# Feed-forward stages: GpSimd starts its scaled inputs with the stage, instead of after the last low part of the normed inputs

## The chip, the cores and the metric

The kernel runs on one core of a Trainium2 chip. The metric is the time of one execution on the device, in microseconds (us), lower is better. A core has five engines that run side by side, each through its own list of instructions: TensorE (PE in the profile; PEld is its weight load) for matrix products, VectorE (DVE) and ScalarE (ACT) for element-wise work, GpSimd (POOL) for element-wise work too, and SyncE (SP), which here issues the transfers. They wait for each other by semaphores: an instruction adds to one when it is done, another engine waits until it has reached a value.

## What is computed

Two small language-model blocks in sequence, on 512 tokens plus 16 learned ones (528 in the first block), width 1024, all in float32. The change concerns the feed-forward part, which comes twice, once in each of the two layers of the first block (hidden width 4096, `ff_up` and `ff_down` of each layer):

```python
for layer in range(DEPTH):                       # DEPTH = 2
    hn = rms_norm(h, attn_norm[layer])
    mix = gated_deltanet(...) if layer == 0 else mlstm(...)
    h = h + mix
    h = h + squared_relu_mlp(rms_norm(h, ffn_norm[layer]), ff_up[layer], ff_down[layer])
...
def squared_relu_mlp(h, w_up, w_down):
    a = jax.nn.relu(h @ w_up)
    return (a * a) @ w_down
```

A third block (gates, attention, one more projection) follows and gives the output.

## The kernel before

The program is a sequence of stages, each a block with one instruction list per engine and a barrier at its end: load and transpose the tokens, the first mixer (three stages), feed-forward 0 (called with name ffn0), the second mixer, feed-forward 1 (ffn1), the last block. Features lie on the 128 partitions, tokens along the free dimension, so `h` is 8 tiles of 128 x 528 (128 x 512 from feed-forward 1 on, where the 16 learned tokens are dropped).

Products keep float32 accuracy with three passes: every operand x is split into a high part (ScalarE copies it to a shorter format, `xhi`) and a low part (VectorE subtracts, `xlo` = x - `xhi`), and TensorE computes whi·xhi + whi·xlo + wlo·xhi.

Both feed-forward stages are `up_down` (line 284), with n = 8 groups of 512 hidden features. For group 0 the up product is plain: two weight units (256 columns each), each times all 8 tiles of the normed input (`unit_tiles`, matmuls of line 196). From group 1 on it is done by a scheme of 7 block products in place of 8 (forms f = 0 to 6 in `up_form`, matmuls of line 663): weight blocks and inputs are first added and subtracted. The mixed inputs are made once per stage: GpSimd multiplies `h` by the gain, tile by tile (line 372, eight instructions, each 128 x 528), and then makes four sums and differences of half blocks (lines 375, 378, 381, 384, each twice as long; each waits for the one before). ScalarE takes their high parts (`t_high`, line 397), VectorE their low parts (`t_low`, line 511). Forms 2, 3, 4 and 6 of the first weight unit need them.

What stands around it at the start of the stage, engine by engine, in the order of each list:

- ScalarE: eight high parts of the gained input (line 938), two squares (941), the high part of weight unit 1 (158), the norm's logarithm and exponential (946, 949), then `cast_up(0,0)`, `cast_up(0,1)` (405), two openings from PSUM (715), a square and a high part of hidden tile 0 (431, 434), `cast_up(0,2)`, `cast_up(0,3)`, the same for hidden tile 1, `t_high` of forms 2, 3, 4, two more openings, `cast_up(0,4)`, `t_high(6)`, `cast_up(0,5)`, square and high part of hidden tile 2, and then `keep` (line 426), which copies the first form's result out of PSUM.
- VectorE: eight low parts of the gained input (line 954), three sums of the norm (962), the low part of weight unit 1 (165), four weight sums (545 to 553), and then thirteen instructions of which four are the low parts of the mixed inputs: `low_up` twice (513), scaling of hidden tiles 0 and 1 (726, twice), low part of hidden tile 0 (557), `low_up` twice, low part of hidden tile 1, `t_low` of 2, 3 and 4, `low_up`, `t_low(6)`. Then comes the scaling of hidden tile 2 (line 726, the third of its kind).
- TensorE: group 0's two units (line 196, with four matmuls of line 970 for the norm between the seventh and eighth input tile of the first), then the forms. Form 2 waits for the low part of its mixed input, form 3 for that and for `keep` of form 0:

```python
if f in (3, 5, 6):
    pe.wait_ge(s.kept, 8 * g + 4 * ub + {3: 1, 5: 2, 6: 3}[f])
```

GpSimd's list of this stage holds nothing but the twelve instructions named. Its results `y` lie in memory that `ahi` and `alo` use from group 1 on. Its inputs are `h` and the gains, both complete before the stage begins. The first line of its list waits until all eight low parts of the normed inputs (`norm.lo`, counted up by line 954) are done.

Of the kernel before, what the change touches and what calls it, by code (L numbers as in the profile page):

```python
# [25 lines left out]
KD = D // P  # L26
# [257 lines left out]
def up_down(k, name, n, up_cols, w_down, activate, acc, norm, then, last_norm):  # L284
# [8 lines left out]
    with ExitStack() as ctx:  # L293
# [54 lines left out]
        @block.sync  # L348
        def _(sp):
            def down(g, j):  # L350
                return wide(w_down, g * 512, 512 * j)
            norm.sync(k, sp)
            def first():
                for j in range(loaded, 2):
                    load_unit(k, sp, u0 + j, up_cols(0, j), (u0 + j) % RAW_SLOTS)
            def step(g, par):
                for j in range(2):
                    if not (zero(g) and 2 + j < loaded):
                        load_unit(k, sp, step_unit(g) + j, up_cols(g + 1, j), slot(j))
                for j in range(2):  # L360
                    load_unit(k, sp, step_unit(g) + 2 + j, down(g, j), slot(2 + j))
            def last():
                for j in range(2):
                    load_unit(k, sp, step_unit(n - 1) + j, down(n - 1, j), slot(j))
            steps(sp, n, step, first, last)
            load_ahead(k, sp, u0 + 4 * n, then)

        @block.gpsimd
        def _(pool):
            pool.wait_ge(norm.lo, KD)  # L370
            for t in range(KD):
                pool.tensor_scalar((y_low if t < 4 else y_high)[:, t % 4, k.now], norm.src[:, t, k.now],
                                   norm.gain[:, t:t + 1], None, ALU.mult).then_inc(s.y_made, 1)
            pool.wait_ge(s.y_made, KD)
            pool.tensor_tensor(y_low[:, :, first_half], y_low[:, :, second_half], y_low[:, :, first_half], ALU.subtract)\
                .then_inc(s.t_made, 1)
            pool.wait_ge(s.t_made, 1)
            pool.tensor_tensor(y_low[:, :, second_half], y_high[:, :, second_half], y_low[:, :, second_half], ALU.subtract)\
                .then_inc(s.t_made, 1)
            pool.wait_ge(s.t_made, 2)  # L380
            pool.tensor_tensor(y_high[:, :, second_half], y_high[:, :, second_half], y_low[:, :, first_half], ALU.subtract)\
                .then_inc(s.t_made, 1)
            pool.wait_ge(s.t_made, 3)
            pool.tensor_tensor(y_high[:, :, first_half], y_high[:, :, second_half], y_high[:, :, first_half], ALU.subtract)\
                .then_inc(s.t_made, 1)
# [4275 lines left out]
```

## Time and profile before

| | |
|---|---|
| time, median of 3 runs | 1918.23 us (1918.07 to 1919.24) |
| profiled execution, its own time | 1919.47 us |
| its span, first to last instruction | 1917.8 us |
| TensorE busy | 1834.2 us, 96% of the span |
| VectorE busy | 1261.2 us, 66% |
| ScalarE busy | 965.0 us, 50% |
| GpSimd busy | 167.5 us, 9% |
| mean granted TensorE clock | 0.980 of full |
| feed-forward 0 begins | at 613.7 us of the span |
| feed-forward 1 begins | at 1233.0 us |

The profile gives, for one execution, when each instruction began and how long it lasted; idle time before an instruction stands in square brackets with the instruction that ended it. Full TensorE clock is 2.4 GHz, the lower level is 1.2 GHz. A duration includes the time in which an instruction that has begun is held up.

### The profile page before, as it was taken

The page shows a single profiled execution, that of the slowest core. Times are in us where ns is not written, and L with a number is a line of the kernel's source. Part 1 is how long each engine was busy: PE and PEld are TensorE (multiplying, and loading weights), DVE is VectorE, ACT ScalarE, POOL GpSimd, SP SyncE. Part 2 cuts the span into 40 slices and gives each one's busy share as a digit, 9 for nine tenths or more (in the row PEclk, how much of TensorE's full clock was granted, in tenths as well). Part 3 has the DMA queues.
Part 4 walks back from the last instruction along what each step waited for, and adds up shares of the span by engine and source line. Part 5 has one row for each costly group of instructions (what it writes and reads, how often), then busy time and mean ns, then how long its engine had stood idle before and what let it go on. Part 6 is the DMA issues. An engine that isn't in the chain of part 4 may idle for free. (4 is left out here: it accounts for less than half of the span.)

```text
span 1917.8 us, 33607 instructions
## 1 busy us (share of the span) xinstructions
PE 1834.2 (96%) x13026; PEld 1671.9 (87%) x13026; DVE 1261.2 (66%) x2235; ACT 965.0 (50%) x1787; POOL 167.5 (9%) x166
## 2 busy tenths in 40 slices
PE   7999999999899799999999999979999998999998
PEld 7999999899699799999999977768889985788776
DVE  6666689986744777777664276567777757863444
ACT  6557763667733544444444366364444433424662
POOL 0001140000000500000000020140000002000101
PEclk9999999999999899999999999989999998999999
DMA  8223462255442133233232232223332332321101
GB/s 203 85 77 118 127 196 59 71 150 164 113 99 67 50 105 111 88 95 103 89 90 89 64 86 79 89 65 107 105 93 88 110 110 68 111 67 45 45 23 44
DMA packets 209652, 179.61 MB, mean 94 GB/s; under 512 B 42544, under 2 KB 181808, under 8 KB 209512
## 3 DMA queue, kind: packets, MB, share of 16 engines
q1 hardware_dynamic: 209512, 177.68, 31.4%
q8 instruction: 95, 1.56, 0.3%
q14 instruction: 45, 0.37, 0.1%
HBM read 164.10 MB, written 13.54 MB: 93 GB/s over the span
## 5 line engine op out<-in xcount | busy, mean ns | idle before, releaser
L196 PE MATMUL ps<-ffn_alo,main_whi 128*128 128x264 f32 (+1 forms) x768 | 205.7, 322 | 0.0
L196 PE MATMUL ps<-ffn_ahi,main_wlo 128*128 128x264 f32 (+1 forms) x768 | 205.1, 321 | 0.0
L196 PE MATMUL ps<-ffn_ahi,main_whi 128*128 128x264 f32 (+1 forms) x768 | 204.7, 321 | 0.0
L196 PE MATMUL ps<-gdn_xhi,gdnf_whi 128*128 128x264 f32 x768 | 160.4, 290 | 4.2 <-DVE gdnf_wlo L1558 4.2
L513 DVE TENSOR_TENSOR main_wlo<-raw,main_whi 128x512 fp32r<-128x512 f32 x212 | 145.0, 686 | 24.8 <-ACT main_whi L405 13.5
L196 PE MATMUL ps<-gdn_xlo,gdnf_whi 128*128 128x264 f32 x768 | 156.1, 285 | 0.0
L196 PE MATMUL ps<-gdn_xhi,gdnf_wlo 128*128 128x264 f32 x768 | 156.0, 284 | 0.0
L575 DVE TENSOR_TENSOR h<-h,ps 128x528 f32<-128x528 f32 (+1 forms) x128 | 89.0, 696 | 88.1 <-PE ps L196 87.5
L165 DVE TENSOR_TENSOR main_wlo<-raw,main_whi 128x2048 fp32r<-128x2048 f32 x38 | 88.1, 2320 | 80.5 <-ACT main_whi L158 80.5
L196 PEld LDWEIGHTS ps<-ffn_ahi,main_whi 128*128 128x128 f32 x768 | 127.8, 188 | 11.2
L196 PEld LDWEIGHTS ps<-ffn_alo,main_whi 128*128 128x128 f32 x768 | 127.5, 188 | 11.0
L196 PEld LDWEIGHTS ps<-ffn_ahi,main_wlo 128*128 128x128 f32 x768 | 127.5, 188 | 10.9
L663 PE MATMUL ps<-ffn_xhi,main_wlo 128*128 128x264 f32 (+1 forms) x448 | 126.5, 282 | 0.0
L663 PE MATMUL ps<-ffn_xhi,main_whi 128*128 128x264 f32 (+1 forms) x448 | 126.2, 282 | 0.0
L663 PE MATMUL ps<-ffn_xlo,main_whi 128*128 128x264 f32 (+1 forms) x448 | 126.2, 282 | 0.0
L196 PEld LDWEIGHTS ps<-gdn_xhi,gdnf_whi 128*128 128x128 f32 x768 | 120.7, 190 | 5.5 <-DVE gdn_xlo L1545 4.4
L1447 DVE SCALAR_TENSOR_TENSOR gdn_y<-gdnf_pre,gdnf_convw,gdn_y 128x528 f32<-128x528 f32 x96 | 82.6, 862 | 59.4 <-ACT gdn_y L1420 57.1
L196 PEld LDWEIGHTS ps<-gdn_xlo,gdnf_whi 128*128 128x128 f32 x768 | 119.6, 189 | 0.0
L196 PEld LDWEIGHTS ps<-gdn_xhi,gdnf_wlo 128*128 128x128 f32 x768 | 119.3, 189 | 0.0
L663 PE MATMUL ps<-ffn_thi,main_whi 128*128 128x264 f32 (+1 forms) x336 | 97.0, 289 | 21.9 <-ACT wide L426 20.4
L405 ACT CAST main_whi<-wide 128x512 fp32r<-128x512 f32 x112 | 69.3, 621 | 81.1 <-PE ps L196 81.0
L405 ACT CAST main_whi<-raw 128x512 fp32r<-128x512 f32 x84 | 52.0, 621 | 107.3 <-PE ps L196 107.2
(556 smaller groups left out, 4909.4 us busy)
## 6 DMA issues: line engine op xcount, KB each, us to landing
raw<-in_ff_up_dram SPq DMA_DIRECT2D x32, 1024.0 KB, 5.5
raw<-in_ff_down_dram SPq DMA_DIRECT2D x32, 1024.0 KB, 5.0
raw<-in_gdn_in_dram SPq DMA_DIRECT2D x24, 1024.0 KB, 6.0
raw<-in_w_in_dram SPq DMA_DIRECT2D x14, 1024.0 KB, 5.3
raw<-in_mlstm_in_dram SPq DMA_DIRECT2D x12, 1024.0 KB, 5.2
raw<-in_gdn_out_dram SPq DMA_DIRECT2D x8, 1024.0 KB, 6.6
gdn_zr<-gdn_z_spilled SPq DMA_DIRECT2D x26, 264.0 KB, 3.0
gdn_v_spilled<-gdn_o SPq DMA_DIRECT2D x16, 264.0 KB, 2.3
```

The lines of the kernel that those rows point to most:

```text
L165: eng.tensor_tensor(k.wlo[:, s, :], k.raw[:, slot, :], k.whi[:, s, :].bitcast(F32), ALU.subtract).then_inc(k.lo_done, 1)
L196: mm = pe.matmul(ps[:, b, 0:k.width], w, x[:, half], start=first and n == 0, stop=last and n == 2)
L405: nc.scalar.copy(whi[:, i % 8, :, :], up_weights(ub, f)).then_inc(k.hi_done if f == 6 else s.hi_part, 1)
L513: return dve.tensor_tensor(wlo[:, i % 8, :, :], src, whi[:, i % 8, :, :].bitcast(F32), ALU.subtract)
L575: dve.tensor_tensor(parted(k, acc[:, j, k.now]), parted(k, acc[:, j, k.now]), filled(k, k.ps[j % 4]), ALU.add).then_inc(s.down_free, 1)
L663: mm = pe.matmul(bank(ub, f), w[:, i % 8, kt, :], y[:, kt, :], start=f in (0, 1, 2, 4) and kt == 0 and x == 0, stop=kt == KD // 2 - 1 and ...
L1447: dve.scalar_tensor_tensor(out=self.y[:, b, :], in0=self.pre[:, b, i:i + T], scalar=self.w[:, i, j:j + 1], in1=self.y[:, b, :], op0=ALU.mu ...
```

## The change

GpSimd's list in both feed-forward stages loses its first line, the wait. Everything else, on every engine, stays.

```diff
         @block.gpsimd
         def _(pool):
-            pool.wait_ge(norm.lo, KD)
             for t in range(KD):
                 pool.tensor_scalar((y_low if t < 4 else y_high)[:, t % 4, k.now], norm.src[:, t, k.now],
                                    norm.gain[:, t:t + 1], None, ALU.mult).then_inc(s.y_made, 1)
```

## Rows read from the trace of the kernel before

**Rows 1.** The page: TensorE's busy share and granted clock, tenths in 40 slices.
```profile
PE   7999999999899799999999999979999998999998
PEclk9999999999999899999999999989999998999999
```

**Rows 2.** Waits in 612 to 722 and 1231 to 1341: total us, times, longest.
```profile
PE ps L663 <- ACT wide L426: 10.3, 1, 10.3
...
PE ps L663 <- ACT wide L426: 10.1, 1, 10.1
```

**Rows 3.** Timeline, feed-forward 0, ScalarE: start, us, instructions, [idle before <-releaser].
```profile
613.73 5.13 ACT L938 ACTIVATE ffn_xhi<-h,gains 128x528 fp32r<-128x528 f32 x8 [10.24 <-PEq L99]
...
646.75 1.07 ACT L397 CAST ffn_thi<-ffn_y 128x1056 fp32r<-128x1056 f32 x1 [4.89 <-POOL ffn_y L381]
...
656.02 0.37 ACT L426 COPY wide<-ps 128x264 f32<-128x264 f32 x1
```

**Rows 4.** Timeline, feed-forward 0, GpSimd.
```profile
620.11 18.08 POOL L372 TENSOR_SCALAR ffn_y<-h,gains 128x528 f32<-128x528 f32 x8 [276.90 <-DVE ffn_xlo L954]
638.28 2.47 POOL L375 TENSOR_TENSOR ffn_y<-ffn_y 128x1056 f32<-128x1056 f32 x1
...
643.37 3.35 POOL L381 TENSOR_TENSOR ffn_y<-ffn_y 128x1056 f32<-128x1056 f32 x1
646.79 2.41 POOL L384 TENSOR_TENSOR ffn_y<-ffn_y 128x1056 f32<-128x1056 f32 x1
```

**Rows 5.** Timeline, feed-forward 0, VectorE.
```profile
614.49 5.52 DVE L954 SCALAR_TENSOR_TENSOR ffn_xlo<-h,gains,ffn_xhi 128x528 fp32r<-128x528 f32 x8 [1.06 <-ACT ffn_xhi L938]
...
622.50 2.28 DVE L165 TENSOR_TENSOR main_wlo<-raw,main_whi 128x2048 fp32r<-128x2048 f32 x1
624.70 1.11 DVE L545 TENSOR_TENSOR wide<-raw 128x512 f32<-128x512 f32 x1
625.74 0.68 DVE L547 TENSOR_TENSOR wide<-raw 128x512 f32<-128x512 f32 x1
...
630.53 1.29 DVE L513 TENSOR_TENSOR main_wlo<-raw,main_whi 128x512 fp32r<-128x512 f32 x2 [2.48 <-ACT main_whi L405]
...
641.89 2.52 DVE L511 TENSOR_TENSOR ffn_tlo<-ffn_y,ffn_thi 128x1056 fp32r<-128x1056 f32 x1 [5.09 <-ACT ffn_thi L397]
...
652.83 1.26 DVE L511 TENSOR_TENSOR ffn_xlo<-ffn_y,ffn_xhi 128x1056 fp32r<-128x1056 f32 x1 [0.28 <-ACT ffn_xhi L397]
654.01 1.32 DVE L726 TENSOR_TENSOR wide<-wide,rinv 128x528 f32<-128x528 f32 x2
```

**Rows 6.** Timeline, single GpSimd scalings of line 372: held up, and alone.
```profile
622.11 4.06 POOL L372 TENSOR_SCALAR ffn_y<-h,gains 128x528 f32<-128x528 f32 x1
...
628.39 1.60 POOL L372 TENSOR_SCALAR ffn_y<-h,gains 128x528 f32<-128x528 f32 x1
```

**Rows 7.** Timeline, first mixer: VectorE's three-operand form alone, and beside GpSimd.
```profile
34.87 0.77 DVE L1447 SCALAR_TENSOR_TENSOR gdn_y<-gdnf_pre,gdnf_convw,gdn_y 128x528 f32<-128x528 f32 x1
...
37.16 1.46 DVE L1447 SCALAR_TENSOR_TENSOR gdn_y<-gdnf_pre,gdnf_convw,gdn_y 128x528 f32<-128x528 f32 x1
```

**Rows 8.** Timeline, feed-forward 0, TensorE: norm, and after the gap.
```profile
627.26 1.05 PE L970 MATMUL ps<-wide,ones 128*128 128x264 f32 x4
...
656.53 0.56 PE L663 MATMUL ps<-ffn_thi,main_whi 128*128 128x264 f32 x1 [10.32 <-ACT wide L426]
```

**Rows 9.** Stretch of 10 us: busy us by engine, PEclk, DMA share, GB/s.
```profile
652.00:662.00 10.00, 5.47 (x30) 5.50 (x31) 9.69 (x16) 7.20 (x15) 0.00 (x0) 0.57 0.05 10
```

**Rows 10.** Timeline, feed-forward 1: GpSimd, VectorE (line 513, then 726).
```profile
1239.29 18.11 POOL L372 TENSOR_SCALAR ffn_y<-h,gains 128x512 f32<-128x512 f32 x8 [76.66 <-DVE ffn_xlo L954]
...
1248.94 1.29 DVE L513 TENSOR_TENSOR main_wlo<-raw,main_whi 128x512 fp32r<-128x512 f32 x2 [1.82 <-ACT main_whi L405]
...
1272.78 1.28 DVE L726 TENSOR_TENSOR wide<-wide,rinv 128x512 f32<-128x512 f32 x2
```

**Rows 11.** Timeline, start of the second mixer: GpSimd's first instruction.
```profile
986.34 0.20 POOL L3095 MEMSET ml_below<- 128x128 f32 x1 [337.13 <-POOLq L99]
```

## Prediction before the result

> **What bounds the kernel now.** I read the page first: TensorE is busy in nearly every slice at full clock, so only a stretch in which TensorE stands still can give time; in the 40 slices apart from the first, the busy digit dips to 7 in the 14th (623 to 671 us) and in the 27th (1247 to 1294 us) [rows 1]. These are the first tens of microseconds of feed-forward 0 and of feed-forward 1. Second, who waited for whom in the 110 us behind each start: TensorE stood still once for 10.3 us and once for 10.1 us, each time before a form of line 663, until ScalarE's copy of line 426 [rows 2]. Nothing else of this size stands in those stretches. Third, the timelines there, followed backwards from the end of the gap. TensorE resumes with form 3 at 656.53 [rows 8]. It needs `keep` of form 0, which begins at 656.02 [rows 3]. The form that it copies was ready long before; `keep` is late since it stands in ScalarE's list behind the square of hidden tile 2, which waits for VectorE's third scaling of line 726 at 654.01, and that stands in VectorE's list behind the low parts of the four mixed inputs, the last at 652.83 [rows 5]. Those follow ScalarE's high parts, and the one at 646.75 had waited 4.89 us for GpSimd's line 381 [rows 3]. GpSimd works without a pause from 620.11 to the end of line 384 at 649.20, and before 620.11 it waits for the last low part of line 954 [rows 4]. So the wait that is taken out does stand at the head of the chain that ends TensorE's gap, in both stages.
>
> **The start of GpSimd.** Without the wait GpSimd begins with the stage. ScalarE begins at 613.73 [rows 3]; at the start of the second mixer GpSimd's first instruction is at 986.34, level with the others [rows 11]. I take 613.8, which is 6.3 us before 620.11. In feed-forward 1 the scalings begin at 1239.29 [rows 10]; by the same distance behind the block's start at 1233.0 I take 6.2 us. If nothing stood in the way, TensorE's form 3 would come as much earlier: 12.5 us in all. That is the far end, not the forecast, because GpSimd's work moves on top of VectorE's.
>
> **What GpSimd and VectorE cost each other.** A scaling alone takes 1.60 us; another, begun at 622.11, took 4.06 [rows 6], and it ends 1.4 us after VectorE's 2.28 us subtraction of line 165 has ended [rows 5]. Behind that subtraction, the sum of line 545 took 1.11 us where the next, of the same size, took 0.68 [rows 5]. So a scaling waits until VectorE's running instruction has ended, and then holds up VectorE's next one by 1.11 - 0.68 = 0.43 us, not by its whole 1.60. With two inputs it is more: the low part at 641.89 took 2.52 us, the like one at 652.83 took 1.26; it began while GpSimd still ran line 378, and line 381 behind it took 3.35 us in place of 2.47 [rows 4, 5]. They take turns, one instruction each. The three-operand form of line 954, beside which GpSimd never runs in these stages, takes its turn too: the same form in the first mixer took 1.46 us beside a GpSimd sum, 0.77 alone [rows 7].
>
> The Trainium skill, "SBUF — State Buffer", section "Who interferes with whom", says that a VectorE instruction with two SBUF inputs and a GpSimd instruction that reads SBUF exclude each other for the whole instruction. The rows for GpSimd's sums agree (a wait until the other has ended), the row for the scalings does not: 0.43 us of hindrance for 1.60 us of instruction. Read literally for the scalings too, the rule speaks against this change; that is the third rival below.
>
> **The scalings, moved.** The first runs before VectorE has anything to do (613.8 to 615.4). The others meet the eight low parts, one per 5.52 / 8 = 0.69 us [rows 5]. Each waits for the end of the running one, holds up the next by 0.43, and comes back 1.6 us later, so to a boundary at 0.43 + 2 x 0.69 = 1.8 us; behind them come the norm's sums and the 2.28 us of line 165, which costs one of them up to 2 us more. Bounds for eight: 8 x 1.8 = 14.4 us, and the 18.08 of today [rows 4]. I take 16.3, nearer to the middle, since one long wait is sure: scalings done at 630.1, where they end at 638.2 now.
>
> VectorE pays at most 7 x 0.43 = 3.0 us for these, about 1 of which it pays already. Its four weight sums end at 628.05 now (630.53 less 2.48 of idle [rows 5]), so at 630.0 then, and its next instruction, which waits for ScalarE, is at 630.53: hidden, with 0.5 us left; without that cover 1 us at most would be lost. TensorE needs the norm's sums at 627.26 [rows 8] (now ended before 622.5, where line 165 begins [rows 5]) and line 165 about 2 us later (now ended at 624.78): 2 us later each is hidden as well. TensorE's first unit wants a low part every 1.5 us (12 matmuls of 0.12), and 0.69 + 0.43 = 1.1 us is less. The very first low part at 614.49 could be held up by the end of GpSimd's first read: 0 to 0.43 us at TensorE's start, taken as 0 because the scaling has been reading for 0.4 us by then.
>
> **From 630.5 on VectorE is what counts.** From the first line 513 to the third scaling of line 726 it has 13 instructions: nine of 128 x 528 or less at 0.62 us from start to start, and four low parts of mixed inputs at 1.17 (durations 0.65 and 1.26 less the overlap with the next). That is 9 x 0.62 + 4 x 1.17 = 10.3 us; it takes 654.01 - 630.53 = 23.5 us now, the rest being waits for GpSimd's results. With the change GpSimd's four sums fall into this stretch from its beginning, and each takes its turn between two of VectorE's. What a sum holds is bounded by 1.9 us (2.47 less half a microsecond until it reads) and 2.4 us (2.41 and 2.47 whole [rows 4]); I take 2.3, the row of line 384 being the nearest. Sum: 10.3 + 4 x 2.3 = 19.5 us, less 0.3 for the part of the first sum before 630.53. The third line 726 is then at 630.53 + 19.2 = 649.7 in place of 654.01: 4.3 us earlier. GpSimd's last sum is done near 642 (630.1 + 4 x 2.45 + 4 x 0.6 of turns), and ScalarE's remaining high parts and copies take 4 us from there: they do not come last. From line 726 to form 3 it stays 656.53 - 654.01 = 2.5 us. So form 3 starts at 652.2. Form 2 waits a little longer than now for its first low part, which changes nothing, since form 3 ends the gap.
>
> In feed-forward 1 the same: nine at 0.605 and four at 1.14 make 10.0 us, four sums of 128 x 1024 at 2.25 make 9.0. From 1248.94 this gives 1267.9, in place of 1272.78 [rows 10]: 4.8 us earlier.
>
> **Sum.** 4.3 + 4.8 = 9.1 us. All that follows in these stages hangs on TensorE, on weight buffers that TensorE frees, or on loads that these release, so it moves as a whole, and later stages begin at a barrier. TensorE's clock: in 652 to 662 it was granted 0.57 of full after the gap [rows 9], which is the 1.2 GHz level for some 4 us, and cost about 2 us; with a gap of 5 to 6 us I expect that again and count nothing. The profiled execution takes 1919.47 us, so it would take 1910.4; that execution lay 1.2 us above the median of the runs shown, 1918.23, which gives 1909.1.
>
> **Rivals.**
> First, the full shift. GpSimd and VectorE hinder each other less than in rows 4 and 5, or the shorter gap spares the drop of the clock: 12.5 us without hindrance, up to 4 more by the clock, so 1902 to 1906. For it speaks only that half of GpSimd's scalings would find VectorE's list short; against it the turns seen in each of GpSimd's overlaps. Chance 0.12.
>
> Second, GpSimd is locked out: the eight low parts of line 954 follow each other without a gap, and if GpSimd does not get a turn between them, only the first scaling (1.6 us) is won, per stage. That is 3.2 us: 1915.0, hardly to be told from no change. Against it: at the end of line 165 VectorE had the next instruction ready as well, and GpSimd did get its turn [rows 5, 6]. That the change does nothing because GpSimd starts late for another reason would look the same. Chance 0.08.
>
> Third, the slower side: a scaling holds VectorE for its whole 1.60 us, from the first low part on. It decides where a low part plus a scaling takes longer than the 1.5 us that TensorE spends per input tile; at 0.69 + 1.60 = 2.3 us it would. The eighth low part would then be at 614.5 + 8 x 2.3 = 632.9; sums of the norm, line 165 and the weight sums add 1.9 + 2.2 + 2.4, then 10.3 + 9.2: the third line 726 at 658.9, 4.9 us later than now, in both stages. 1928. The Trainium skill's rule above, taken for the scalings too, gives this. Against it the 0.43 us of line 545. Chance 0.04.
>
> **Chances and range.** The forecast with its terms has 0.73, the first rival 0.12, the second 0.08, the third 0.04, and 0.03 is left for the unforeseen. The bounds: with 1.9 us per sum of GpSimd the gain is 9.1 + 8 x 0.4 = 12.3; with 2.4, scalings of 18 us and 1 us lost at each start it is near 5. I take 1905.0 to 1914.4. A measurement can tell about 0.2% from no change, 3.8 us, so faster means below 1914.4. Faster 0.87 (forecast, first rival, a part of the rest), same 0.08, slower 0.05.
>
> **What would show it.** Line 372 begins within 0.3 us of the stage, its eight instructions take 15 to 18 us, and several instructions of line 954 last about 1.2 us. The four sums begin near 630 and each is followed by one lengthened VectorE instruction of 513, 726 or 557. The third line 726 is near 649.7 and 1267.9, and TensorE's wait for line 426 shrinks from 10.3 to about 5 us. Wrong would be: TensorE waiting in its first unit for line 954, or the third line 726 where it is now; then the turns cost what the start gave.

## The result

| | before | changed |
|---|---|---|
| median | 1918.15 us (1917.11 to 1920.92, 6 runs) | 1906.68 us (1905.08 to 1912.48, 6 runs) |
| profiled execution, its own time | 1919.47 us | 1905.67 us |
| its span | 1917.8 us | 1904.0 us |
| mean granted clock | 0.980 | 0.986 |

The ratio is 0.9945, with a 95% interval of 0.993 to 0.9961: 11.5 us faster by the medians, 7.5 to 13.4 us by the interval. 9.1 had been forecast, and a time of 1905.0 to 1914.4 us. One execution of the kernel before, beside the last experiments, took 3593.21 us and is left out of their comparisons.

**Where it went, by stage.** The start of a stage is the start of ScalarE's first or GpSimd's first instruction in it; the differences, in us, from the profiled executions:

| | before | changed |
|---|---|---|
| feed-forward 0, start to start of the second mixer | 372.6 | 368.7 |
| second mixer (not changed) | 246.7 | 243.9 |
| feed-forward 1 | 365.0 | 360.2 |
| behind feed-forward 1 (not changed) | 319.8 | 317.3 |

3.9 + 4.8 = 8.7 us lie in the two stages that were changed, and 2.8 + 2.5 = 5.3 in code that the change does not touch; the experiments come back to these.

**Feed-forward 0 after the change.** GpSimd's timeline; lines of the file are one less than before. It answers to [rows 4].

```profile
613.83 17.50 POOL L371 TENSOR_SCALAR ffn_y<-h,gains 128x528 f32<-128x528 f32 x8 [271.35 <-POOLq L99]
631.41 2.81 POOL L374 TENSOR_TENSOR ffn_y<-ffn_y 128x1056 f32<-128x1056 f32 x1
634.30 2.81 POOL L377 TENSOR_TENSOR ffn_y<-ffn_y 128x1056 f32<-128x1056 f32 x1
...
640.10 2.82 POOL L383 TENSOR_TENSOR ffn_y<-ffn_y 128x1056 f32<-128x1056 f32 x1
```

GpSimd begins with the stage (ScalarE's first instruction is at 613.80). Each sum lasts 2.82 us in place of the 2.47 or less that one takes alone, and behind it follows the next at once.

VectorE's timeline in the same place (answers to [rows 5]):

```profile
614.57 6.79 DVE L953 SCALAR_TENSOR_TENSOR ffn_xlo<-h,gains,ffn_xhi 128x528 fp32r<-128x528 f32 x8 [1.07 <-ACT ffn_xhi L937]
...
630.59 1.29 DVE L512 TENSOR_TENSOR main_wlo<-raw,main_whi 128x512 fp32r<-128x512 f32 x2 [1.21 <-ACT main_whi L404]
631.80 5.88 DVE L725 TENSOR_TENSOR wide<-wide,rinv 128x528 f32<-128x528 f32 x2
637.60 2.98 DVE L556 TENSOR_TENSOR ffn_alo<-wide,ffn_ahi 128x528 fp32r<-128x528 f32 x1
640.51 3.56 DVE L512 TENSOR_TENSOR main_wlo<-wide,main_whi 128x512 fp32r<-128x512 f32 x2
...
644.61 3.58 DVE L510 TENSOR_TENSOR ffn_tlo<-ffn_y,ffn_thi 128x1056 fp32r<-128x1056 f32 x3
...
649.88 1.31 DVE L725 TENSOR_TENSOR wide<-wide,rinv 128x528 f32<-128x528 f32 x2
```

The eight low parts cost 6.79 us in place of 5.52. From 630.59 on VectorE is never idle: the two scalings that took 1.75 us together now take 5.88, because two of GpSimd's sums take their turns there, and two more sit in the next two rows. The third scaling is at 649.88.

TensorE in feed-forward 0, the matmul after each idle stretch among the forms (answers to [rows 8]), and its longest wait in 1225 to 1335, feed-forward 1 (answers to [rows 2]):

```profile
645.95 0.36 PE L662 MATMUL ps<-ffn_thi,main_whi 128*128 128x264 f32 x1 [1.48 <-issue]
...
652.40 0.56 PE L662 MATMUL ps<-ffn_thi,main_whi 128*128 128x264 f32 x1 [4.75 <-ACT wide L425]
```

```profile
PE ps L662 <- ACT wide L425: 4.2, 1, 4.2
```

The gap of 10.3 us has become one of 4.75 and a new one of 1.48 ahead of form 2, in feed-forward 1 4.2 and 2.8 in place of 10.1 and 1.4. (Where a row says "issue", the profile shows nothing that the engine waited for; form 2's code waits there for its low part, the first of the three at 644.61.)

### The profile page after: what moved, and what is told of

Its sections match the earlier page's. It is cut to its first block and busy times, and to the rows that moved or that the text cites. A ratio compares the mean times of both kernels' runs of the same rounds, so it can differ in the third digit from the quotient of the medians.

```text
span 1904.0 us, 33607 instructions
## 1 busy us (share of the span) xinstructions
PE 1826.9 (96%) x13026; PEld 1665.8 (87%) x13026; DVE 1273.9 (67%) x2235; ACT 963.8 (51%) x1787; POOL 167.1 (9%) x166
## 3 DMA queue, kind: packets, MB, share of 16 engines
q1 hardware_dynamic: 209512, 177.68, 31.7%
## 5 line engine op out<-in xcount | busy, mean ns | idle before, releaser
L512 DVE TENSOR_TENSOR main_wlo<-raw,main_whi 128x512 fp32r<-128x512 f32 x212 | 144.9, 685 | 21.2 <-ACT main_whi L410 10.3
```

The source lines that it names most:

```text
L512: return dve.tensor_tensor(wlo[:, i % 8, :, :], src, whi[:, i % 8, :, :].bitcast(F32), ALU.subtract)
```

## The experiments

**The changed kernel again, and the wait taken out in one layer alone.** What would separate the change's own gain from the 5.3 us in unchanged code.

> The changed kernel once more. In its first profiled execution the span was 13.8 us shorter than that of the kernel before, of which 3.9 lie in feed-forward 0, 4.8 in feed-forward 1, and 5.1 in the stages behind them, which are unchanged. Theory A (turns on VectorE): the change is worth 8 to 9 us, in the feed-forward stages; the rest are drops of TensorE's clock to 1.2 GHz that fall in some executions and not in others. Then the median is 8 to 12 us below the kernel before, feed-forward 0 again gives 3.8 to 4.3 us from its start to the start of the next stage, and some of the 5 us in the unchanged stages is gone or moved elsewhere. Rival B: the unchanged stages gain by the shift itself; then the start of the second mixer to the start of feed-forward 1 is again 244.0 us (246.7 before) and feed-forward 1's end to the end of the program again 2.5 us shorter than before.

```diff
         @block.gpsimd
         def _(pool):
+            if last_norm:
+                pool.wait_ge(norm.lo, KD)
             for t in range(KD):
```

> The wait is taken out in feed-forward 0 alone and stays in feed-forward 1. Theory A: feed-forward 0 is as in the changed kernel (third scaling of hidden tiles about 36 us behind the stage's start, TensorE's gap there 4.8 us), feed-forward 1 as in the kernel before (39.7 us behind its start, gap 10 us); the time is 4 to 5.5 us below the kernel before, 1913 to 1914.5. Rival B (the unchanged stages gain by being shifted): 6 to 8 us below, since the second mixer and the last block are shifted too.

| | feed-forward 0 | second mixer | feed-forward 1 | behind it |
|---|---|---|---|---|
| changed, again | 368.6 | 244.4 | 360.4 | 319.8 |
| layer 0 alone | 368.7 | 244.1 | 364.5 | 319.8 |

Medians, with the runs of the kernel before on the same chip at 1919.44: changed again 1908.9 (ratio 0.9937, 0.9923 to 0.9951), layer 0 alone 1913.24 (0.9966, 0.9953 to 0.9979). The feed-forward stages repeat to 0.2 us. The part behind them is back at 319.8, so its 2.5 us were no gain of the change. The second mixer stays near 244, which still fits both theories. Nor does the time tell them apart: 6.2 us by the medians lies where rival B had it (6 to 8) and above theory A's 4 to 5.5, and its interval, 4.0 to 9.0 us, holds both. With the wait back in feed-forward 1 that stage is at 364.5; its third scaling comes 39.4 us behind its start (39.7 before), its gap ahead of form 3 is 9.8 us. Half of the change is there: 3.9 us in feed-forward 0. The second mixer's 246.7 - 244.1 adds 2.6.

**The kernel before twice more, and the changed one a third time.** Files unchanged; only the question of the second mixer.

> The kernel before, profiled again. The two feed-forward stages took 372.6 and 365.0 us in its first profile, the second mixer 246.7, and the part behind feed-forward 1 319.8. If drops of TensorE's clock are what makes the unchanged stages differ between executions (theory C), the feed-forward stages repeat within 1 us, and the second mixer and the last part may come out at 244 or 317.3 as they did in an execution of the changed kernel, each difference going with one more or one less stretch at 1.2 GHz. If instead the change itself makes the second mixer shorter (rival B), it is 246.7 again.

> The kernel before, a third profile, for the same question: theory C, feed-forward stages 372.6 and 365.0 within 1 us, the second mixer either 244 or 246.7 according to the clock; rival B, 246.7.

> The changed kernel, a third profile. Feed-forward 0 368.6 and feed-forward 1 360.3 us within 0.5, VectorE's third scaling of hidden tiles 36.1 us behind the start of feed-forward 0. Theory C: the second mixer 244 or 246.7 according to the clock; rival B: 244 again.

| | feed-forward 0 | second mixer | feed-forward 1 | behind it | time |
|---|---|---|---|---|---|
| before, again | 372.4 | 246.7 | 364.9 | 319.8 | 1919.39 |
| before, third | 372.5 | 246.7 | 364.9 | 319.8 | 1921.48 |
| changed, third | 367.9 | 246.7 | 360.9 | 320.0 | 1913.44 |

Rival B had said 246.7 for the kernel before, and so it came; but the changed kernel's third execution has the second mixer at 246.7 too, so a shift of the stage does not by itself make it shorter: rival B falls. (Its feed-forward 0, 367.9, is 0.2 us outside what was expected; the third scaling is 36.0 us behind the start.) The whole second mixer in the changed kernel's first profile and in its third (columns: us, busy us of PE, PEld, DVE, ACT, POOL, granted clock, DMA share, GB/s):

```profile
982.54:1226.47 243.93, 234.83 (x1494) 204.24 (x1494) 131.46 (x305) 118.43 (x248) 19.59 (x24) 0.99 0.30 84
```

```profile
984.17:1230.83 246.66, 237.58 (x1494) 206.84 (x1494) 131.23 (x305) 118.90 (x249) 17.60 (x24) 0.98 0.30 83
```

The same 1494 matmuls kept TensorE busy for 2.75 us longer, and the stage is 2.73 us longer: the difference is TensorE's clock. It sits in two places. In the ten microseconds that begin 135 us and 165 us behind the mixer's start the granted clock was 0.83 in the third profile, as in the kernel before, and 1.00 in the first; 0.83 over 10 us is 3.4 us at 1.2 GHz and full clock otherwise. Behind feed-forward 1 it is the same: TensorE was busy for 304.3 us in the kernel before and for 301.8 in the changed kernel's first profile, with 1764 matmuls in both.

That the kernel before showed 246.7 in all three of its profiles was allowed by theory C but not what it would lead one to expect. The experiments below add to the count. Of the eight profiles in which GpSimd begins with feed-forward 0, five have the mixer at 243.9 to 244.4, one at 245.2 and two at 246.7 and 246.8; the four in which it begins later (the three of the kernel before, and the half-way one) have 246.7 each. So the change may make these two drops rarer, which would be worth more than the 8.7 us; these profiles are too few to settle it.

**GpSimd's sums made narrow.** How much of what is left is their turns on VectorE?

```diff
+            first_few, second_few = (slice(x.start, x.start + 16) for x in (first_half, second_half))
             pool.wait_ge(s.y_made, KD)
-            pool.tensor_tensor(y_low[:, :, first_half], y_low[:, :, second_half], y_low[:, :, first_half], ALU.subtract)\
+            pool.tensor_tensor(y_low[:, :, first_few], y_low[:, :, second_few], y_low[:, :, first_few], ALU.subtract)\
                 .then_inc(s.t_made, 1)
...
```

> The four sums of GpSimd are made over 16 columns of each half block only; the rest of the mixed inputs is left uncomputed. Scalings as in the changed kernel. Theory A (VectorE's list plus GpSimd's turns is the bound): without the four turns of about 2.3 us, VectorE's third scaling in feed-forward 0 comes at 644 to 645.5 in place of 649.9 (then limited by ScalarE, whose opening of hidden tile 3 waits for TensorE until 641.4), and TensorE's gap ahead of form 3 falls from 4.8 us to 1 to 2.5 us. If the sums cost VectorE nothing (rival: only the order of GpSimd's results counts), the third scaling comes no earlier than 649, because VectorE's and ScalarE's lists are unchanged.

This kernel leaves most of the mixed inputs uncomputed and ran once (1895.46 us); only its timeline is of use.

The stage begins at 616.34 here. VectorE's third scaling, and TensorE's matmul after its only gap of the forms:

```profile
645.98 1.32 DVE L726 TENSOR_TENSOR wide<-wide,rinv 128x528 f32<-128x528 f32 x2
...
648.50 0.36 PE L663 MATMUL ps<-ffn_thi,main_whi 128*128 128x264 f32 x1 [1.57 <-ACT wide L426]
```

645.98 - 616.34 = 29.6 us behind the start, where the changed kernel has 36.1: 6.4 us earlier, half a microsecond beyond the expected 644 to 645.5, which are 30.2 to 31.7 behind 613.8. VectorE's and ScalarE's lists are the same, so the rival (only the order of results counts) falls. But not all of the 6.4 us is the sums. VectorE's first line 513 began at 631.85, 15.5 us behind the start in place of 16.8; from there to the third scaling it is 14.1 us in place of 19.3, so the sums cost 5.2 us net. Their four turns came to 9.0; without them VectorE stands idle for 2.75 us in this stretch, waiting for ScalarE.

The other 1.3 us are the clock's. It stayed at 2.4 GHz (1.00 granted over 615 to 625 and over 645 to 655) through the 2.7 us of idle TensorE at the stage's start and through the gap of 1.57. TensorE makes the norm's column sums early in the stage, ScalarE's work on them stands ahead of its casts of the weight blocks, and VectorE's line 513 waits for the first cast. With 1.00, 0.83 and 0.66 granted over the first ten microseconds of feed-forward 0 that line began 15.2 (the half-way kernel), 16.8 (before, changed) and 18.0 us (the last experiment) behind the start. Feed-forward 0 took 360.1 us, 8.6 less than in the changed kernel: 4.7 of gap (4.75 + 1.48 - 1.57) and 4.0 by the clock, for TensorE was busy for 355.5 us in place of 359.4. Feed-forward 1 took 350.6.

**GpSimd begins half-way.**

```diff
         @block.gpsimd
         def _(pool):
+            pool.wait_ge(norm.lo, 4)
             for t in range(KD):
```

> GpSimd's first wait comes back, but for four low parts instead of eight, so GpSimd begins some 3.6 us behind the stage's start instead of 6.4 (before) or 0.1 (changed). Theory A (VectorE's own 10.3 us and GpSimd's four turns fill the time up to the third scaling of line 726): as long as the sums begin before VectorE runs dry, the start of GpSimd hardly matters; the third scaling comes 36.8 to 37.3 us behind the stage's start (40.3 before, 36.1 changed). Rival (the gain follows GpSimd's start in proportion): 38.3 us or later.

```profile
618.26 19.48 POOL L372 TENSOR_SCALAR ffn_y<-h,gains 128x528 f32<-128x528 f32 x8 [276.06 <-DVE ffn_xlo L954]
637.83 2.47 POOL L375 TENSOR_TENSOR ffn_y<-ffn_y 128x1056 f32<-128x1056 f32 x1
```

```profile
653.56 1.32 DVE L726 TENSOR_TENSOR wide<-wide,rinv 128x528 f32<-128x528 f32 x2
```

I was wrong here: the third scaling is at 653.56 - 614.59 = 39.0 us behind the start, not at 37. GpSimd began 2.7 us earlier than before but its scalings took 19.5 us, not 17.5, and its sums began only when VectorE had run dry (its low part at 641.44 came after 5.09 us of idle time). From the first sum to the third scaling it is 15.73 us, to the hundredth what it was before (638.28 to 654.01). The time is in the rival's range (38.3 or later), but the gain did not follow GpSimd's start in proportion either: that would be 38.5 (2.7 of 6.4 us of lead, so 1.8 of 4.2). So there are two bounds: GpSimd's first sum plus 15.7 us, and VectorE's serial list with the turns. Of the change's 4.2 us, the last half of GpSimd's lead brought 2.9; VectorE's list was the bound with the whole of it and not with the half. The kernel ran once, in 1917.61 us.

**The sums held back.** Are the turns a waste?

```diff
             pool.wait_ge(s.y_made, KD)
+            pool.wait_ge(s.lo, 2)
```

> The changed kernel, but GpSimd's first sum waits until VectorE has made the low part of hidden tile 1, so that no sum takes a turn among the eight instructions ahead of that. Theory A: the turns are work that has to be done anyway on a shared path, and keeping them out of a busy stretch only puts VectorE's idle time behind it: the sums begin 22.3 us behind the stage's start (24.5 before, 17.6 changed), the third scaling comes 2 to 2.5 us earlier than before, 38 us behind the start, which is later than the changed kernel's 36.1. Rival (the turns cost more than they give, the change throws time away there): the third scaling at 36 us or less.

```profile
636.85 2.47 POOL L375 TENSOR_TENSOR ffn_y<-ffn_y 128x1056 f32<-128x1056 f32 x1 [5.66 <-DVE ffn_alo L557]
```

```profile
633.73 0.71 DVE L557 TENSOR_TENSOR ffn_alo<-wide,ffn_ahi 128x528 fp32r<-128x528 f32 x1 [0.76 <-ACT ffn_ahi L434]
...
652.61 1.32 DVE L726 TENSOR_TENSOR wide<-wide,rinv 128x528 f32<-128x528 f32 x2
```

The third scaling is at 652.61 - 613.67 = 38.9 us behind the start, 2.9 later than in the changed kernel and 1.3 earlier than before (2 to 2.5 had been expected, since I took the start of the sums 0.9 us too early). VectorE's early instructions are short again (0.71 us for line 557 in place of 2.98) and it pays with idle time later. The rival falls: to let the sums take turns is worth 2.9 us. 15.76 us lie between the first sum and the third scaling, nearly the 15.73 of before. The kernel ran once, in 1912.8 us.

**ScalarE's copy moved forward.** If `keep` is late only by its place in the list, it can be moved.

```diff
                 cast_up(0, 5)
+                keep(0, 0, 0, 0, 1, 1)
                 squared(0, 2)
                 hi_tile(0, 2, 0)
...
-                    if ub < 2 and f == 0:
+                    if ub < 2 and f == 0 and not (zero(g) and ub == 0):
                         keep(g, ub, f, 0, 1, 1)
```

> The changed kernel, and in addition ScalarE copies the result of the very first form out of PSUM (keep) before the square and the high part of hidden tile 2 instead of behind them, in both stages. If the reading of the chain is right (keep is late only because of its place in ScalarE's list, behind a square that waits for VectorE), form 3 starts at 647.5 in place of 652.4 and the 4.8 us gap ahead of it vanishes; VectorE's list is unchanged, so TensorE then waits ahead of form 5, whose low part VectorE makes at 653.6: a gap of about 3.5 us there. Net 2 to 2.5 us per stage, plus up to 2 if the clock stays up: 4 to 7 us below the changed kernel. Rival: form 3 does not move, because something else holds it (its mixed input or its weight's low part); then the time is that of the changed kernel.

```profile
645.69 0.36 PE L663 MATMUL ps<-ffn_thi,main_whi 128*128 128x264 f32 x1 [1.46 <-issue]
...
654.39 0.56 PE L663 MATMUL ps<-ffn_xhi,main_whi 128*128 128x264 f32 x1 [4.01 <-ACT wide L425]
```

```profile
653.87 0.37 ACT L425 COPY wide<-ps 128x264 f32<-128x264 f32 x1
```

The gap ahead of form 3 is gone (it begins at 647.23), and one of 4.01 us stands ahead of form 5. What ended it was not VectorE's low part, as expected, but ScalarE again: form 5 waits for `keep` of form 2 too, which ended at 654.24, and the low part of its weight block, begun at 653.39, had ended at 654.07. That copy stands in ScalarE's list behind the square of hidden tile 3. In feed-forward 0 this gave only 0.4 us (368.3): over 652 to 662 the granted clock was 0.66, in the changed kernel 0.73. In feed-forward 1 the gap ahead of form 5 was 2.28 us, the clock over 1256 to 1266 was 0.83 against 0.60, and it gave 2.3 us (357.9). The median is 1905.43 (1904.73 to 1906.8), against 1908.9 for the changed kernel on the same chip; ratio to before 0.9924, 0.9912 to 0.9937. The intervals of the two overlap (0.9923 to 0.9951), so that it beats the changed kernel is not shown: it is 3.5 us by these medians, less than the 4 to 7 expected, and 1.3 against the changed kernel's first median, 1906.68.

**Both lists in TensorE's order.** The work is the same, its order is what TensorE asks for.

```diff
+                cast_up(0, 2)
+                cast_up(0, 3)
                 squared(0, 0)
                 hi_tile(0, 0, 0)
-                cast_up(0, 2)
-                cast_up(0, 3)
...
                 cast_up(0, 5)
+                keep(0, 0, 0, 0, 1, 1)
+                cast_up(0, 6)
+                keep(0, 0, 2, 1, 2, 3)
+                for m in range(2, 4):
+                    open_tile(m)
...
                 t_low(6, 4)
+                low_up(0, 5)
+                low_up(0, 6)
+                lo_tile(0, 0, 0)
+                lo_tile(0, 1, 0)
```

> The changed kernel with the lists of ScalarE and VectorE at the start of the stage in the order in which TensorE asks: weight blocks 2 and 3 before the squares, the copies of forms 0 and 2 and the high part of block 6 before the openings of hidden tiles 2 and 3, and VectorE's low parts of blocks 5 and 6 before the low parts of hidden tiles 0 and 1 and the scalings. The work is the same. Theory A: the bound is VectorE's serial list with GpSimd's turns, so what comes last is what stands last: no gap over 1 us ahead of forms 3, 5 and 6; the next wait is ahead of the second unit's first form, which needs 18 short and 4 long instructions and four turns, 11.0 + 4.7 + 9.2 us behind 630.6, 655.5 in place of 660.5 in the changed kernel. 4 to 5 us less per stage: 8 to 10 us below the changed kernel. Rival: ScalarE's list becomes what comes last, and no more is won than with the copy alone moved (2 to 3 us in all).

TensorE's matmuls after idle time, in a stage that begins at 618.60, and the copy that ended the longest wait:

```profile
654.61 0.36 PE L670 MATMUL ps<-ffn_thi,main_whi 128*128 128x264 f32 x1 [1.28 <-DVE main_wlo L517]
...
662.76 0.36 PE L670 MATMUL ps<-ffn_xhi,main_whi 128*128 128x264 f32 x1 [3.55 <-ACT wide L425]
```

```profile
662.25 0.37 ACT L425 COPY wide<-ps 128x264 f32<-128x264 f32 x1
```

The expectation failed, and what it named as its rival is what the rows show. There is a gap of 1.07 us ahead of form 2 (at 651.62), one of 1.28 ahead of form 3 and one of 3.55 ahead of form 6, 5.9 in all where the changed kernel has 6.2; none stands ahead of the second unit. (By count of the matmuls, twelve to a form: form 5 begins at 657.60, form 6 at 662.76.) Form 6 waits for `keep` of form 3, which is ScalarE's copy at 662.25; it was left behind the squares and high parts of hidden tiles 2 and 3, which wait for VectorE's scalings, now later in its list (the third one 39.4 us behind the start). The first form of the second unit begins at 664.56, 46.0 us behind the start, where 41.7 had been expected and the changed kernel has 46.7.

The profiled execution is moreover not a typical one. It took 1915.9 us; of the six executions, only one was longer (1917.11), and the other four lie at 1902.84 to 1906.85. It had feed-forward 0 at 369.3 us and feed-forward 1 at 361.3, both a little more than the changed kernel; the first ten microseconds of both were granted 0.66 of the clock, where the changed kernel had 0.83 and 1.00. The median is 1906.61, ratio 0.9933 (0.991 to 0.9955). The 8 to 10 us did not come, and the order alone is not shown to be worth anything over the copy moved forward.

## Why the prediction was right, point by point

- **The bound and the chain.** Right. TensorE's gap was ended by `keep`, `keep` by the third scaling, that by VectorE's list. From the third scaling to form 3 it is 652.40 - 649.88 = 2.5 us as said, and moving `keep` moved form 3 from 652.40 to 647.23.
- **GpSimd's start.** Right. 613.83 measured, 613.8 said; in feed-forward 1 GpSimd begins level with the block too.
- **The cost of a scaling to VectorE.** Right. The three low parts that were held up lasted 1.12 to 1.21 us against 0.76, so 0.36 to 0.45 us each (0.43 said), and all eight 6.79. What the Trainium skill's "Who interferes with whom" in "SBUF — State Buffer" says of the whole instruction holds here, nearly, for the two-input sums (2.25 us for 2.47 of instruction), and not for the one-input scalings (0.36 to 0.45 for 1.60). The third rival, built on that, is refuted by the same rows.
- **The scalings.** 17.5 us, 16.3 said: the range was 14.4 to 18.1. They ended at 631.33, so no part of the first sum lay ahead of VectorE's stretch, where 0.3 us had been counted. They were 1.2 us late and it did not matter, since VectorE still had work of its own when the first sum came.
- **VectorE's list from 630.5.** 649.88 - 630.59 = 19.3 us; 19.2 said. With 10.3 us of its own the four turns come to 9.0, 2.25 each; 2.3 said. (The prediction's lower bound for a turn, 1.9, takes off half a microsecond "until it reads"; no run shows that half microsecond.) The third scaling: 649.88 against 649.7. In feed-forward 1 34.4 us behind the start, 34.9 said; 35.0 in the third profile, where the clock fell at the stage's start as in the kernel before (0.83 over the first ten microseconds, 1.00 in the first profile).
- **The sum.** 4.3 + 4.8 = 9.1 said for the two stages, 3.9 + 4.8 = 8.7 measured, and 8.6 and 8.8 with the changed kernel's second and third profiles against the same first profile before (8.3 and 8.6 against the second and third). Form 3 came 4.2 us earlier behind the start of feed-forward 0 (38.6 for 42.8) and the stage gave 3.9: after the shorter gap the matmuls ran at 1.2 GHz for 4.8 us (652.40 to 657.2), after the longer one for 3.9 (656.53 to 660.4). The prediction's reading of 0.57 as "some 4 us" is right for the time in which TensorE worked; the whole 0.57 is 8.6 us at the lower level, over half of it idle.
- **What was missing.** "All that follows moves as a whole" was right for the work and wrong for the clock. In the first pair 5.3 us of 13.8 lie in the second mixer and behind feed-forward 1, where the same matmuls took TensorE 2.8 and 2.6 us less. In the medians, 11.5 and 10.5 us, some 2 to 3 us are above what the two stages gave; the second mixer's 2.3 to 2.8 us in two of three profiles is of that size. The prediction named the clock only for the gap itself. That the median came out 11.5 us lower and not 9.1 is therefore in part luck of the clock, or an effect of the change on it that nobody foresaw; it stays open which.
- **The first rival.** The profiled time, 1905.67, lies in its range (1902 to 1906), but not for its reasons: the turns cost what the forecast had, and the clock fell again after the shorter gap. **The second rival** falls with the low parts of 1.12 to 1.21 us: GpSimd did get its turns between them.
- **The other bound.** GpSimd's results could have come last. The prediction looked at that (last sum near 642, four more microseconds, so 646) and rightly put it aside: the last sum ended at 642.92, and with the 15.7 us of the kernel before from first sum to third scaling it would be 631.41 + 15.7 = 647.1, against 649.9. The expectation for the half-way experiment took for granted that the sums would begin before VectorE ran dry. They did not, since the scalings took 19.5 us, and it failed by 2 us.

## What to carry to other kernels

A wait at the head of a helper engine's list that guards no data is worth its length only up to the point where the next engine's own list fills the time; add that list up, with what the helper takes from it in turns, and compare with the chain of the helper's results: the later of the two is the forecast. When a copy that frees TensorE stands behind work that waits for something else, moving it hands most of the gap to the next form (4.75 us became 4.01, and 4.2 became 2.28 in the other stage). And compare stages, not spans, with TensorE's busy time beside each: between two executions of one file the clock alone moved unchanged stages by 2 to 3 us each.

## What the runs showed of the hardware

A one-input GpSimd instruction of 128 x 528 (1.6 us) holds up a VectorE instruction with two SBUF inputs by about 0.4 us; a two-input sum of 128 x 1056 (2.47 us alone) by 2.25, and itself lasts 2.82 when a VectorE instruction of 0.6 us takes its turn between two. Both wait for the running instruction of the other to end: the scaling that met the 2.28 us of line 165 took 4.08 us, wherever in the list it stood (the sixth in the changed kernel, the third in the half-way one).

TensorE idle for 2.7 us at a stage's start was followed by a drop to 1.2 GHz in the changed kernel's feed-forward 0 (0.83 granted over the first ten microseconds), by more of it in the last experiment (0.66) and by none in the changed kernel's feed-forward 1, in the half-way kernel or with narrow sums (1.00): the same idle time has either outcome. In the second mixer, two such drops of 3.4 us each cost 2.7 us together.
